# Gate and up products of a feed-forward stage, given to four PSUM banks in turn

## The chip, the cores and the metric

The kernel runs on one core of a Trainium2 chip. The metric is the time of one execution on the device in microseconds (us). Before the change three runs took 1269.52, 1270.49 and 1271.22 us, so the median is 1270.49 us. The names used for the engines are PE for TensorE (PEld for its weight loads), DVE for VectorE, ACT for ScalarE, POOL for GpSimd and SP for SyncE, which issues the weight transfers.

## The reference

The program is one inference step of a trunk of two layers, for 256 prompt tokens and 64 sample tokens (320 together) that share their weights. Each layer mixes tokens in two branches, and ends in the feed-forward part that the change is in:

```python
h = _rmsnorm(x, p['norm_ffn_pre'])
f = (jax.nn.silu(h @ p['w_ffn_gate']) * (h @ p['w_ffn_up'])) @ p['w_ffn_down']
x = x + _rmsnorm(f, p['norm_ffn_post'])
```

The model's width is 1024 and that of the feed-forward part 2816. Everything is float32.

## The kernel before

**Layout.** Features lie on the partitions and the 320 tokens on the free axis, so that a projection is a set of products of a 128x128 weight block (loaded into PE) with a 128x320 block of activations (streamed through it). The width of 1024 is 8 such blocks, k = 0 to 7, and that of 2816 is 22.

**Three products for one.** To keep float32 accuracy, a weight tile is split into a high part `w_hi`, made by ACT (line 599), and a low part `w_lo`, made by DVE (line 912), and activations likewise into `h_hi` and `h_lo`. Every block pair takes three products in the same sum: hi x hi, hi weight x lo activation, lo weight x hi activation. `parts` (line 1404) gives them in this order. A weight tile has 1024 columns, so 8 blocks and 24 products. Raw, high and low tiles lie in rings of three: SP loads a raw tile when the low part of the tile three before it has been made, and ACT makes a high part when PE has used the tile three before.

**The gate and up stage.** There are 11 quads per layer (`q` in `for q in range(FK // 2)`). A quad makes four sums of 128x320, gate, up, gate, up: group g+0, g+1, g+2, g+3. Each has a PSUM bank of its own and 24 products (8 values of k by 3). The quad consumes four weight tiles in four calls of `cycle`, each of which takes two values of k for all four sums: 24 products per cycle, 96 per quad. Within a cycle the sums are taken in the order 0, 2, 1, 3, and each gets its six products (two k, three parts) in one piece. In the first quad of a layer (`ready` is given) the order is by k first, since the activations arrive one k at a time: there each sum gets three products in one piece.

**Banks.** Seven banks go round: `wide = dense + core[1:5]`, and `bank(g)` is `wide[(g - G_GU) % 7]`. Quad 1 so has core2, core3, core4, dense0 for its sums 0 to 3, quad 2 has dense1, dense2, core1, core2. The first product into a bank waits (`open_bank`, line 1390) until the group seven before has been read out of it. For the sums 0, 1 and 2 of a quad that is a group of the quad before last; for sum 3 it is sum 0 of the quad just before.

**Reading out.** DVE multiplies each finished sum by the norm's `root` into SBUF (line 1359), in the order 0, 2, 1, 3, and counts `dense_evac_v`. The last value of k of each sum in a cycle counts `phase_done`, so a quad counts 16. `finished` (line 343) makes the reading of sums 0 and 2 wait for the 15th count of the quad, that of sums 1 and 3 for the 16th. ACT applies SiLU to the gates (line 885), and DVE multiplies by the up sum, splits the result into `f_hi` and `f_lo` (lines 1365, 939, 940), and makes low parts of four weight tiles in between. Then it waits for the next quad.

**Around it.** Behind the first quad, PE does one product with `pick` (`x_pick`), ACT makes `root` from it (lines 632, 634), and only then can DVE read out the first quad. After quad 10 the down projection uses `f_hi` and `f_lo` in 22 tiles, with all 66 products of an output group in one bank.

All matmuls are recorded at line 1388, the helper `mm`.

Of the kernel before, what the change touches and what calls it, by code (L numbers as in the profile page):

```python
# [10 lines left out]
T = TP + TS  # L11
# [11 lines left out]
T_WOA, T_WOB, T_WO, T_GU, T_DOWN, NT = 55, 59, 67, 75, 119, 141  # L23
# [123 lines left out]
def program(nc, x_t, wts, pvec, lora, shift0, fixed, rmask, trig, rconst, wkv_st, ret_d, ret_t,  # L147
# [5 lines left out]
    with ctx:  # L153
# [95 lines left out]
        def bank(g):  # L249

            if g < OPEN:
                return opened[g]
            if T_V <= g < T_GATE + 4:
                return dense[(g - T_V) % 2]
            return dense[(g - (OPEN if g < T_V else T_GATE + 4)) % 3] if g < G_GU else wide[(g - G_GU) % 7]
# [11 lines left out]
        def many(n, *names, unit=1):  # L267

            return [Signal(name, n, unit) for name in names]
# [9 lines left out]
        phase_done, = many(4 * (T_DOWN - T_GU), "phase_done")  # L279
# [53 lines left out]
        def low_ready(layer, n):  # L333

            return low_made(layer, n + 1)
# [23 lines left out]
        def evacuated_by(layer, g):  # L359

            if T_V <= g < T_GATE:
                return v_feat(layer, g - T_V + 1)
            if G_GU <= g < G_DOWN:
                g += (0, 1, -1, 0)[(g - G_GU) % 4]
            on_dve = [q < T_QK or T_GATE <= q < G_WO or G_GU <= q < G_DOWN for q in range(g + 1)]
            return dense_evac_v(layer, sum(on_dve)) if on_dve[g] else dense_evac_a(layer, sum(not v for v in on_dve) - 8 * (g >= T_GATE))
# [5 lines left out]
        def ch(t, c, lo=0, hi=T):  # L372
            return t[:, c * T + lo:c * T + hi]
# [1009 lines left out]
        def _(pe):  # L1383
            pe.wait_ge(fixed_loaded, 16)
            pe.wait_ge(pad_ready, 2)
            for layer in range(DEPTH):
                def mm(out, lhsT, rhs, start=True, stop=True):
                    return pe.matmul(out, lhsT, rhs, start=start, stop=stop)  # L1388

                def open_bank(g):  # L1390
                    if g >= G_GU + 7:
                        pe.wait_ge(*evacuated_by(layer, g - 7))
                    elif g >= G_GU:
                        pe.wait_ge(*evacuated_by(layer, G_GU - 1))
                        if g >= G_GU + 4:
                            pe.wait_ge(*ret_upd_evac(layer, 2 * HP))
                    elif g == T_GATE + 6:
                        pe.wait_ge(*seq_evac(layer, EVAC_AT["s3", SAMPLE]))
                    elif T_V + 2 <= g < T_GATE + 6:
                        pe.wait_ge(*evacuated_by(layer, g - 2))  # L1400
                    elif g >= OPEN and (V_FIRST or g not in (T_V, T_V + 1)):
                        pe.wait_ge(*evacuated_by(layer, g - (OPEN if g < OPEN + 3 else 3)))

                def parts(j, b):

                    hi, lo = w_hi[j % RING][:, b * 128:(b + 1) * 128], w_lo[j % RING][:, b * 128:(b + 1) * 128]
                    return ((hi, 0), (hi, 1), (lo, 0))
# [105 lines left out]
                def halves(out, lhsT, rhs, start=True, stop=True):  # L1513

                    mm(out[0:C], lhsT[0:C], rhs[0:C], start, stop)
                    return mm(out[C:2 * C], lhsT[C:2 * C], rhs[C:2 * C], start, stop)

                def across(out, lhsT, rhs, start=True, stop=True):

                    mm(out[C:2 * C], lhsT[0:C], rhs[0:C], start, stop)  # L1520
                    return mm(out[0:C], lhsT[C:2 * C], rhs[C:2 * C], start, stop)
# [24 lines left out]
                def product(job, m):  # L1546

                    name, lv, s = job
                    bank = round_bank(job)
                    b128 = slice((4 * s + m) * 128, (4 * s + m + 1) * 128)  # L1550
                    b64 = slice((4 * s + m) * C, (4 * s + m + 1) * C)
                    of = slice(m * C, (m + 1) * C)
                    ps, ps64 = bank[:, m * 128:(m + 1) * 128], bank[:, of]
                    turned = across if s in FLIP else halves
                    if name == "vt":
                        return across(ps64, stream(zs[:, 11 * T:15 * T], s)[:, m, :], i2)
                    if name == "mt":
                        return halves(ps, b_st[:, b64], ar[:, b128])
                    if name == "kt":
                        return across(ps, k_st[:, b64], ar[:, b128])  # L1560
                    if name == "tk":
                        return across(ps64, k_dec[:, of] if s == HP else k_st[:, b64], i2)
                    if name == "tb":
                        return halves(ps64, b_dec[:, of] if s == HP else b_st[:, b64], i2)
                    if name in ("m", "mx"):
                        return (across if name == "mx" else halves)(ps64, ar[:, b128][:, 0:C], b_st[:, b64])
                    if name == "e":
                        return turned(ps64, (p_sq[lv % 2] if lv else m_sq)[:, b64], xt[:, b64])
                    if name == "dt":
                        return turned(ps64, x_sq[:, b64], e_sq[:, b64])  # L1570
                    return halves(ps64, e_sq[:, b64], x_sq[:, b64])

                pe.wait_ge(*bonus_out(layer, HP))
                for i, slot in enumerate(ROUNDS, 1):
                    pair = [named(t) for t in slot.split()]
                    for job in pair:
                        n = JOB_AT[job] - 1
# [5 lines left out]
                    for m in range(4):  # L1583
                        for job in pair:
                            ins = product(job, m)
# [34 lines left out]
                for name, c in SEQ:  # L1620
                    w, u = (wu_s, wu_s) if c == SAMPLE else (w_st, u_st)

                    def mat(t, h, w):
                        return step_mats(t, c, w)[:, h, :]

                    def out(what, h):
                        b, o = seq_place(what, c)
                        return banks[b][:, o + h * C:o + (h + 1) * C]

                    def col(t, h):  # L1630
                        return t[:, h * C:(h + 1) * C]
# [17 lines left out]
                    if name in ("as0", "as1", "as2", "as3"):  # L1649
# [5 lines left out]
                        for s in range(NSEQ):  # L1655
# [3 lines left out]
                            ins = halves(o3[:, :, toks], col(s0_st, h * NSEQ + s), a3[:, :, toks])  # L1659
                        done(ins)  # L1660
                    elif name == "w":
# [5 lines left out]
                        for h in range(HP):  # L1667
                            beside(h)
                            if c == SAMPLE:
                                ins = halves(out("w", h), asr[:, h * 128:h * 128 + C], i2)  # L1670
                            elif c:
                                ins = halves(out("w", h), mat(ar, h, 128)[:, 0:C], col(s_st, h))
                            else:
                                ins = across(out("w'", h), mat(makt, h, C), mat(v_st, h, C))
                        done(ins)
                    elif name == "u":
                        evac("w", c)
                        for h in range(HP):
                            beside(h)
                            ins = halves(out("u", h), mat(xt, h, C), col(w, h))  # L1680
                        done(ins)
                    elif name in ("ys", "y"):
                        evac("u", c)
                        for h in range(HP):
# [4 lines left out]
                            ins = halves(out("y", h), col(u, h), mat(mrb, h, C), not state, True)  # L1689
                        if name == "ys":  # L1690
                            for h in range(HP):
                                ins = halves(out("s", h), mat(tok, h, 128)[:, C:2 * C], col(u, h))
# [72 lines left out]
                for hp in range(HP):  # L1765
                    q, k = ch(qk_rot, hp), ch(qk_rot, 4 + hp)
# [17 lines left out]
                    for u in range(2):  # L1784
                        for j in range(4):
                            of = slice((2 * j + u) * 128, (2 * j + u + 1) * 128)
                            ins = mm(core[2][32 * j:32 * j + 32, 384:512], q_exp[:, (2 * j + u) * 32:(2 * j + u + 1) * 32],
                                     old[:, of], u == 0, u == 1)
# [13 lines left out]
                    both = core[3][:, TP:TP + 2 * TS]  # L1802
# [21 lines left out]
                def cycle(n, g, k0, last, act, ready=None):  # L1824

                    pe.wait_ge(*low_ready(layer, T_GU + n))
                    both = [(one, k) for one in (0, 2, 1, 3) for k in (k0, k0 + 1)]
                    if ready:
                        both.sort(key=lambda u: u[1])
                    for one, k in both:  # L1830
                        if k == 0:
                            open_bank(g + one)
                        if ready and one == 0:
                            pe.wait_ge(*ready(layer, k))
                        for m, (w, which) in enumerate(parts(T_GU + n, 4 * (k - k0) + one)):
                            ins = mm(bank(g + one)[:, 0:T], w, ch(act[which], k), k == 0 and m == 0, k == last and m == 2)
                        if k == k0 + 1:
                            ins.then_inc(phase_done.sem, 1)

                for q in range(FK // 2):  # L1840
                    for i in range(4):
                        cycle(4 * q + i, G_GU + 4 * q, 2 * i, KT - 1, (h_hi, h_lo),
                              (lambda layer, k: h_ready(layer, KT + k + 1)) if q == 0 else None)
                        if q == 0 and i in (1, 2):
                            x_sum(2, i - 1)
                        if q == 0 and i == 3:
                            x_pick(2)
# [149 lines left out]
```

## Time and profile before

| what | us |
|---|---|
| median of three runs | 1270.49 |
| span of the profiled execution | 1270.8 |
| PE busy | 1221.7 (96% of the span) |
| PE weight loads busy | 1157.7 (91%) |
| DVE busy | 855.3 (67%) |
| ACT busy | 558.2 (44%) |
| PE busy from 416 to 558 us (quads 1 to 10 of the first layer) | 141.58 of 142.00 |

For the profiled execution the page gives the span only; it lies 0.3 us above the median and inside the three runs. Busy means that an instruction is in the engine, and products overlap each other in PE: a 128x320 product is recorded as 0.31 us long, while the next starts about 0.147 us after it. What a product costs is therefore the distance between two starts. Where PE waits, the row of the product carries the idle time and the engine that ended it in square brackets.

### The profile page before, as it was taken

To read this page: it belongs to the slowest core of one execution; us is meant where nothing else is said; L and a number is where in the kernel's file an instruction comes from. 1 tells how busy PE (TensorE), PEld (TensorE's weight loads), DVE (VectorE), ACT (ScalarE), POOL (GpSimd) and SP (SyncE) were. 2 spreads that over 40 slices of the span, in tenths; PEclk is the share of its full clock that TensorE was granted. 3 is DMA by queue.
4 is the path that set the end of the run, shared out by engine and by line. 5 is a ranking of instruction groups with operands and counts; after the bars stand their busy time and mean duration, and the time that the engine had idled before them with its cause. 6 is when DMAs were issued, how large, how long until landed. Compare 5 with 4: busy or idle time off the path is not lost.

```text
span 1270.8 us, 27906 instructions
## 1 busy us (share of the span) xinstructions
PE 1221.7 (96%) x12056; PEld 1157.7 (91%) x12056; DVE 855.3 (67%) x1468; ACT 558.2 (44%) x849; POOL 152.7 (12%) x168
## 2 busy tenths in 40 slices
PE   6999899999999999999989998999999999999996
PEld 5999788998998999999978987889999989999996
DVE  4887558878776666663378864687878576666433
ACT  4553345455536333343355544444563453333432
POOL 0004456100000000000000062840100000000000
PEclk9999899999999999999999999999999999999999
DMA  6433144644453644444424432364444535444441
GB/s 215 143 116 122 40 118 146 250 127 144 123 166 102 221 150 150 150 149 150 150 91 126 134 100 74 103 212 172 148 159 135 163 107 166 152 143 154 153 149 67
DMA packets 51466, 179.13 MB, mean 141 GB/s; under 512 B 6288, under 2 KB 7568, under 8 KB 50064
## 3 DMA queue, kind: packets, MB, share of 16 engines
q1 hardware_dynamic: 42576, 153.77, 38.5%
q10 hardware_dynamic: 8768, 23.58, 5.2%
q8 instruction: 95, 1.56, 0.5%
q14 instruction: 27, 0.22, 0.1%
HBM read 166.18 MB, written 8.53 MB: 137 GB/s over the span
## 4 chain that ended last, share of the span: by engine, by line
PE 83%; DVE 9%; ACT 4%; issue 2%; DMA 1%; ACTq 0%; SPq 0%; DVEq 0%
PE dense L1388 52%; PE core L1388 31%; DVE w_lo L912 2%; ACT w_hi L599 1%; DVE x L962 1%; DVE y_out L960 1%; DMA ret_s<-ret_t 1%; DMA x<-x_t 0%; ACT L587 0%; DVE ret_t L1257 0%; DVE bonus L1031 0%; DVE tmp L1017 0%; ACT sq_pair L822 0%; ACT h_hi L605 0%; DVE bonus L1027 0%
## 5 line engine op out<-in xcount | busy, mean ns | idle before, releaser
L912 DVE TENSOR_TENSOR w_lo<-w_raw,w_hi 128x1024 fp32r<-128x1024 f32 x282 | 352.7, 1253 | 220.1 <-ACT w_hi L599 219.5
L599 ACT ACTIVATE w_hi<-w_raw 128x1024 fp32r<-128x1024 f32 x282 | 297.6, 1057 | 415.5 <-PE dense L1388 273.3
L1388 PE MATMUL dense<-h_hi,w_hi 128*128 128x320 f32 x1296 | 415.3, 320 | 20.1 <-DVE w_lo L912 11.3
L1388 PE MATMUL dense<-h_lo,w_hi 128*128 128x320 f32 x1296 | 403.0, 311 | 0.0
L1388 PE MATMUL dense<-h_hi,w_lo 128*128 128x320 f32 x1296 | 402.8, 311 | 0.0
L1388 PEld LDWEIGHTS dense<-h_hi,w_hi 128*128 128x128 f32 x1296 | 245.5, 189 | 40.2 <-issue 30.8
L1388 PEld LDWEIGHTS dense<-h_lo,w_hi 128*128 128x128 f32 x1296 | 245.9, 190 | 1.3 <-issue 0.2
L1388 PEld LDWEIGHTS dense<-h_hi,w_lo 128*128 128x128 f32 x1296 | 245.7, 190 | 0.0
L1388 PE MATMUL core<-h_hi,w_hi 128*128 128x320 f32 x416 | 129.3, 311 | 0.4 <-DVE w_lo L912 0.4
L1388 PE MATMUL core<-h_hi,w_lo 128*128 128x320 f32 x416 | 128.7, 309 | 0.0
L1388 PE MATMUL core<-h_lo,w_hi 128*128 128x320 f32 x416 | 128.7, 309 | 0.0
L1388 PEld LDWEIGHTS core<-h_hi,w_hi 128*128 128x128 f32 x416 | 78.2, 188 | 0.8 <-DVE w_lo L912 0.7
L1388 PEld LDWEIGHTS core<-h_lo,w_hi 128*128 128x128 f32 x416 | 78.2, 188 | 0.2
L1388 PEld LDWEIGHTS core<-h_hi,w_lo 128*128 128x128 f32 x416 | 78.2, 188 | 0.0
L491 POOL TENSOR_TENSOR xt<-xt,fx 128x256 f32<-128x256 f32 x10 | 7.4, 736 | 558.0 <-DVE xt L1085 558.0
L587 ACT ACT_TABLE_LOAD x31 | 39.8, 1283 | 34.7 <-DMA ret_s<-ret_t 16.2
L1388 PE MATMUL dense<-f_hi,w_hi 128*128 128x320 f32 x176 | 54.2, 308 | 0.0
L1388 PE MATMUL core<-f_lo,w_hi 128*128 128x320 f32 x176 | 54.2, 308 | 0.0
L1388 PE MATMUL core<-f_hi,w_lo 128*128 128x320 f32 x176 | 54.2, 308 | 0.0
L1388 PE MATMUL core<-f_hi,w_hi 128*128 128x320 f32 x176 | 54.2, 308 | 0.0
L1388 PE MATMUL dense<-f_lo,w_hi 128*128 128x320 f32 x176 | 54.2, 308 | 0.0
L1388 PE MATMUL dense<-f_hi,w_lo 128*128 128x320 f32 x176 | 54.2, 308 | 0.0
(306 smaller groups left out, 1994.1 us busy)
## 6 DMA issues: line engine op xcount, KB each, us to landing
w_raw<-wts SPq DMA_DIRECT2D x282, 512.0 KB, 3.5
ret_t<-ret_t ACTq DMA_DIRECT2D x16, 256.0 KB, 3.4
ret_s<-ret_t ACTq DMA_DIRECT2D x16, 256.0 KB, 2.4
ret_rest<-ret_d ACTq DMA_DIRECT2D x2, 1536.0 KB, 8.2
qk_rot<-qk_raw SPq DMA_DIRECT2D x8, 320.0 KB, 6.4
dmask<-rconst ACTq DMA_DIRECT2D x2, 1152.0 KB, 5.4
s_st<-wkv_st ACTq DMA_DIRECT2D x2, 1024.0 KB, 4.9
wkv_s<-s_st ACTq DMA_DIRECT2D x2, 1024.0 KB, 4.3
```

Of the source, the lines that this page charges most:

```text
L491: return pool.tensor_tensor(pairs(t, s, C), pairs(t, s, C), bc(i2, 1, 4), ALU.add)
L587: act.preload_act_table_set(name)
L599: act.activation(w_hi[n % RING][:, :], w_raw[n % RING][:, :], ACT.Copy).then_inc(hi_ready.sem, 1)
L912: dve.tensor_tensor(w_lo[r][:, :], w_raw[r][:, :], w_hi[r][:, :].bitcast(F32), ALU.subtract).then_inc(low_made.sem, 1)
L960: link(dve.tensor_tensor(y.rearrange("p (c t) -> p c t", t=T), y.rearrange("p (c t) -> p c t", t=T), bc(root[:, :], 1, hi - lo), ALU.mult))
L962: dve.tensor_tensor(xs, xs, y, ALU.add).then_inc(added.sem, 1)
L1388: return pe.matmul(out, lhsT, rhs, start=start, stop=stop)
```

## The change

In `cycle` the loops change places. For each of the two values of k, and for each of the three parts, the four sums get one product each, in the order 0, 2, 1, 3. The number of products, their operands and the order within one sum stay; so do the wait for the weight tile at the head of a cycle and the wait for the activations at the head of each k. The wait that opens a bank stands as before in front of the first product into it, and the `phase_done` counts stand behind the last product of each sum in a cycle.

```diff
-                    both = [(one, k) for one in (0, 2, 1, 3) for k in (k0, k0 + 1)]
-                    if ready:
-                        both.sort(key=lambda u: u[1])
-                    for one, k in both:
-                        if k == 0:
-                            open_bank(g + one)
-                        if ready and one == 0:
+                    for k in (k0, k0 + 1):
+                        if ready:
                             pe.wait_ge(*ready(layer, k))
-                        for m, (w, which) in enumerate(parts(T_GU + n, 4 * (k - k0) + one)):
-                            ins = mm(bank(g + one)[:, 0:T], w, ch(act[which], k), k == 0 and m == 0, k == last and m == 2)
-                        if k == k0 + 1:
-                            ins.then_inc(phase_done.sem, 1)
+                        for m in range(3):
+                            for one in (0, 2, 1, 3):
+                                if k == 0 and m == 0:
+                                    open_bank(g + one)
+                                w, which = parts(T_GU + n, 4 * (k - k0) + one)[m]
+                                ins = mm(bank(g + one)[:, 0:T], w, ch(act[which], k), k == 0 and m == 0, k == last and m == 2)
+                                if k == k0 + 1 and m == 2:
+                                    ins.then_inc(phase_done.sem, 1)
```

The instruction lists of DVE, ACT and SP stay as they are. On PE, here is the place where quad 1 of the first layer ends and quad 2 begins, in the kernel before. Quad 1 ends with six products into dense0 (its sum 3), and the last into core3 (its sum 1) is the row ahead of them; quad 2 comes to core2, which holds sum 0 of quad 1, with its 19th product.

```order
L1388 MATMUL core3<-h_hi,w_lo1 128x320
L1388 MATMUL dense0<-h_hi,w_hi1 128x320
L1388 MATMUL dense0<-h_lo,w_hi1 128x320
...
L1388 MATMUL dense0<-h_hi,w_lo1 128x320
L1388 MATMUL dense1<-h_hi,w_hi2 128x320 [waits dense_evac_v,low_made]
L1388 MATMUL dense1<-h_lo,w_hi2 128x320
...
L1388 MATMUL dense2<-h_hi,w_lo2 128x320
L1388 MATMUL core2<-h_hi,w_hi2 128x320 [waits dense_evac_v]
```

The same place after the change, with no row left out:

```order
L1388 MATMUL core2<-h_hi,w_lo1 128x320
L1388 MATMUL core4<-h_hi,w_lo1 128x320
L1388 MATMUL core3<-h_hi,w_lo1 128x320
L1388 MATMUL dense0<-h_hi,w_lo1 128x320
L1388 MATMUL dense1<-h_hi,w_hi2 128x320 [waits dense_evac_v,low_made]
L1388 MATMUL core1<-h_hi,w_hi2 128x320 [waits dense_evac_v]
L1388 MATMUL dense2<-h_hi,w_hi2 128x320 [waits dense_evac_v]
L1388 MATMUL core2<-h_hi,w_hi2 128x320 [waits dense_evac_v]
```

The last product into core3, with the 15th count, has moved from the seventh place before the end of the quad to the second, and the first product into core2, with the wait for its being read, from the 19th place of the next quad to the fourth.

At the end of quad 0 the kernel before goes on, behind `pick`, with six products into core2, six into core4 and six into core3, and then comes to dense0, which holds sum 0 of quad 0. After the change it reads:

```order
L1388 MATMUL core1<-h_hi,w_lo0 128x320
L1388 MATMUL core0<-acc_141,fx 128x320 [waits x_parted]
L1388 MATMUL core2<-h_hi,w_hi1 128x320 [waits ret_upd_evac,dense_evac_a,low_made]
L1388 MATMUL core4<-h_hi,w_hi1 128x320 [waits ret_upd_evac,dense_evac_a]
L1388 MATMUL core3<-h_hi,w_hi1 128x320 [waits ret_upd_evac,dense_evac_a]
L1388 MATMUL dense0<-h_hi,w_hi1 128x320 [waits dense_evac_v]
L1388 MATMUL core2<-h_lo,w_hi1 128x320
```

Here too the product that waits for DVE's reading of dense0 has moved from the 19th place to the fourth.

## Rows read from the trace of the kernel before

**Rows 1.** The page, parts 1 and 4: busy times, and shares of the chain.

```profile
PE 1221.7 (96%) x12056; PEld 1157.7 (91%) x12056; DVE 855.3 (67%) x1468; ACT 558.2 (44%) x849; POOL 152.7 (12%) x168
...
PE dense L1388 52%; PE core L1388 31%; DVE w_lo L912 2%; ACT w_hi L599 1%; DVE x L962 1%; DVE y_out L960 1%; DMA ret_s<-ret_t 1%; DMA x<-x_t 0%; ACT L587 0%; DVE ret_t L1257 0%; DVE bonus L1031 0%; DVE tmp L1017 0%; ACT sq_pair L822 0%; ACT h_hi L605 0%; DVE bonus L1027 0%
```

**Rows 2.** Stretches, gate and up: length, busy PE, PEld, DVE, ACT, POOL, clock, DMA.

```profile
416.00:558.00 142.00, 141.58 (x964) 141.16 (x963) 90.64 (x142) 52.54 (x64) 0.00 (x0) 1.00 0.52 162
1040.00:1181.00 141.00, 141.00 (x962) 140.84 (x961) 90.20 (x141) 52.29 (x63) 0.00 (x0) 1.00 0.48 154
```

**Rows 3.** PE timeline, first products of quads 2 and 3: start, duration, instruction.

```profile
431.10 0.31 PE L1388 MATMUL dense<-h_hi,w_hi 128*128 128x320 f32 x1
...
445.18 0.31 PE L1388 MATMUL core<-h_hi,w_hi 128*128 128x320 f32 x1
```

**Rows 4.** PE timeline in the down projection, two products 96 apart.

```profile
1195.88 0.31 PE L1388 MATMUL core<-f_hi,w_hi 128*128 128x320 f32 x1
...
1209.96 0.31 PE L1388 MATMUL core<-f_hi,w_hi 128*128 128x320 f32 x1
```

**Rows 5.** PE timeline in quad 0, where a bank ends and another begins.

```profile
400.53 0.31 PE L1388 MATMUL dense<-h_lo,w_hi 128*128 128x320 f32 x1
400.68 0.31 PE L1388 MATMUL dense<-h_hi,w_lo 128*128 128x320 f32 x1
400.82 0.31 PE L1388 MATMUL core<-h_hi,w_hi 128*128 128x320 f32 x1
```

**Rows 6.** PE timeline at the end of quad 2 and the head of quad 3.

```profile
444.16 0.31 PE L1388 MATMUL dense<-h_hi,w_lo 128*128 128x320 f32 x1
...
444.89 0.31 PE L1388 MATMUL core<-h_lo,w_hi 128*128 128x320 f32 x1
...
445.62 0.31 PE L1388 MATMUL core<-h_hi,w_hi 128*128 128x320 f32 x1
```

**Rows 7.** DVE timeline around the same place and on through quad 3.

```profile
443.02 1.23 DVE L912 TENSOR_TENSOR w_lo<-w_raw,w_hi 128x1024 fp32r<-128x1024 f32 x1 [2.29 <-ACT w_hi L599]
444.57 0.49 DVE L1359 TENSOR_TENSOR silu_g<-dense,root 128x320 f32<-128x320 f32 x1 [0.33 <-PE dense L1388]
...
453.58 1.23 DVE L912 TENSOR_TENSOR w_lo<-w_raw,w_hi 128x1024 fp32r<-128x1024 f32 x1 [2.29 <-ACT w_hi L599]
```

**Rows 8.** DVE's waits over the whole span: us in total, times, longest.

```profile
DVE silu_g L1359 <- ACT root L634: 5.0, 2, 3.0
DVE silu_g L1359 <- PE core L1388: 4.0, 12, 0.3
DVE silu_g L1359 <- PE dense L1388: 2.6, 8, 0.3
```

**Rows 9.** Timeline of DVE, PE and PEld where PE waits for `w_lo` in quad 1.

```profile
422.68 1.23 DVE L912 TENSOR_TENSOR w_lo<-w_raw,w_hi 128x1024 fp32r<-128x1024 f32 x1 [1.85 <-ACT w_hi L599]
...
423.23 0.31 PE L1388 MATMUL dense<-h_hi,w_lo 128*128 128x320 f32 x1
...
423.96 0.19 PEld L1388 LDWEIGHTS core<-h_hi,w_hi 128*128 128x128 f32 x1 [0.69 <-DVE w_lo L912]
...
424.21 0.31 PE L1388 MATMUL core<-h_lo,w_hi 128*128 128x320 f32 x1
```

**Rows 10.** Timeline of PE, ACT and DVE at the head of quad 1, first layer.

```profile
416.78 0.31 PE L1388 MATMUL core<-h_hi,w_hi 128*128 128x320 f32 x1
...
417.10 0.47 ACT L634 ACTIVATE root<-root 128x320 f32<-128x320 f32 x1
...
417.60 0.89 DVE L1359 TENSOR_TENSOR silu_g<-dense,root 128x320 f32<-128x320 f32 x2 [1.96 <-ACT root L634]
```

**Rows 11.** Timeline of PE and DVE at the same place of the second layer.

```profile
1041.00 0.31 PE L1388 MATMUL core<-h_hi,w_hi 128*128 128x320 f32 x1
...
1041.82 0.89 DVE L1359 TENSOR_TENSOR silu_g<-dense,root 128x320 f32<-128x320 f32 x2 [3.03 <-ACT root L634]
```

**Rows 12.** Stretches with and without a lowered clock, columns as in rows 2.

```profile
146.00:150.00 4.00, 1.68 (x67) 1.38 (x66) 1.06 (x3) 1.16 (x4) 0.00 (x0) 0.88 0.03 8
150.00:154.00 4.00, 4.00 (x69) 3.67 (x72) 0.66 (x3) 0.00 (x0) 0.00 (x0) 0.50 0.02 4
154.00:158.00 4.00, 4.00 (x125) 3.74 (x119) 2.93 (x6) 1.32 (x4) 0.00 (x0) 0.77 0.15 12
396.00:412.00 16.00, 14.00 (x102) 11.52 (x98) 13.67 (x21) 10.87 (x22) 0.00 (x0) 1.00 0.16 54
```

## The prediction

> **What bounds the kernel now.** I read the page first. PE is busy for 1221.7 of 1270.8 us, and 83% of the chain that ended last are its products [rows 1]. The table by stretches then says what holds in the stage that changes: from quad 1 on PE is busy for 141.58 of 142.00 us in the first layer and for all of 141.00 in the second, at a granted clock of 1.00, and DVE for 90 to 91 [rows 2]. The stage is a row of products with nothing between them, so its time is their number times their distance, plus what PE waits. The PE timeline gives the distance: quad 2 starts at 431.10 and quad 3 at 445.18, so 96 products take 14.08 us, or 0.1467 us each [rows 3]. Two things can change it: another distance, or new waits. For the waits I read the timelines of PE and DVE around the end of a quad, where DVE has to read a bank that PE wants again.
>
> **The distance of two products: nothing.** The change adds no product and no weight load. It changes the bank with each product, 96 times a quad, where it was 16 times (every sixth). Whether a change of bank costs or saves can be read from stages that change it at other rates. In the down projection 66 products in a row go to one bank, and 96 of them take 1209.96 - 1195.88 = 14.08 us [rows 4], the same as with 16 changes. Inside quad 0, which changes every third product, the step across a change (400.68 to 400.82) is 0.14 us and that inside a bank (400.53 to 400.68) 0.15 us [rows 5], equal within the 0.01 us of the rows. So 16 changes against one or two make less than 0.01 us, or under 0.001 us per change. The change adds 80 in each of 20 quads and 64 in each of the two first (which go from 32 to 96), 1728 in all: at 0.001 us that is 1.7 us to either side, and I take 0. No row has a change at every product, so this is an extrapolation, and its failure is a rival.
>
> **The wait at the fourth product of a quad: +0.32 us, 18 times.** Two things move toward each other. DVE reads sum 0 when the 15th count of the quad has come. That count is now on the last product of sum 1, the 18th of 24 in the last cycle; it starts at 444.16 [rows 6], and DVE, which has been idle for 0.33 us, starts to read at 444.57 [rows 7], 0.41 us later. After the change the 15th count is on the 23rd product, five places later, which starts at 444.89 [rows 6]. DVE will then start at 444.89 + 0.41 = 445.30 and, with a reading of 0.49 us [rows 7], end at 445.79. The bank of sum 0 is needed by sum 3 of the next quad. Now that is its 19th product, 15 places or 2.2 us after the fourth, and never late; after the change it is the fourth, due at 445.62 [rows 6]. So it is late, and I need what a wait costs beyond the moment of release. PE's wait for `w_lo` shows it: DVE ends at 422.68 + 1.23 = 423.91, the weight load starts at 423.96, and the product after the released one starts at 424.21, so the released one holds the place of 424.21 - 0.15 = 424.06 [rows 9]: 0.15 us behind DVE's end, since the weight load is held up too. The fourth product is worth 445.79 + 0.15 = 445.94 instead of 445.62, a loss of 0.32 us. The bounds: if DVE starts earlier by 0.07 (it wakes sooner behind a stream of counts) and the weight load is not held up (0.05 in place of 0.15), the loss is 0.15; if DVE needs 0.1 more, it is 0.42.
>
> How often: DVE waits for PE ahead of this reading 12 + 8 = 20 times, never by less than the rest, 6.6 us in all or 0.33 each [rows 8]. These are quads 1 to 10 of both layers; DVE is thus on time at every one. Quad 10 is followed by the down projection, which comes to that bank much later; quads 1 to 9 pay: 18 x 0.32 = 5.8 us (2.7 to 7.6).
>
> Behind DVE's reading wait SiLU on ACT and the split of `f` and the next low parts on DVE, all some 0.73 us later than now (five products). It is hidden: later in the quad DVE idles for 2.29 us ahead of a `w_lo`, for a high part that ACT can make only when PE has used a tile [rows 7]. And the last `f` blocks are wanted by the down projection 60 and more products (8.8 us) after the quad's end.
>
> **The first quad: +1.46 us in the second layer, +0.78 in the first.** Here the reading waits not for PE but for `root`, which ACT makes from the product behind quad 0. DVE reads sum 0 from 417.60 on, for 0.49 us, until 418.09 [rows 7, 10]. Neither moves. PE's fourth product of quad 1 stands at 416.78 [rows 10] and now goes into a bank that is free; after the change it wants the bank of sum 0 and gets it at 418.09 + 0.15 = 418.24. The loss is 1.46 us. In the second layer: 1041.82 + 0.49 + 0.15 - 1041.00 = 1.46 us [rows 11]. In the first layer PE loses time in this quad already: after 423.23 the next product is due at 423.38 and holds the place of 424.06 because `w_lo` is late, 0.68 us [rows 9]. That low part waits for ACT, behind SiLU and transfers which all hang on the same reading of quad 0 and don't move; PE, 1.46 us later, finds it ready. So the first layer pays 1.46 - 0.68 = 0.78 us.
>
> **Sum.** 5.8 + 1.46 + 0.78 = 8.0 us. PE is the end of the chain behind the stage too (down projection, next layer), so nothing takes it back. The profiled span of 1270.8 lies 0.3 above the median of 1270.49; on the median that gives 1278.5 us. The likeliest case's own range, from the bounds of the steady wait and of the first quads (0.1 each way), is 1275 to 1280.5 us.
>
> **Rivals.**
> *The products come closer together.* If giving each product another bank than its neighbour lets it start earlier, all 2112 products gain. 320 columns at 2.4 GHz, the level of a granted clock of 1.00 [rows 2], are 133.3 ns, against a distance of 146.7: up to 13.3 x 2112 = 28 us less. With the waits that is 1270.5 + 8 - 28 = 1250 us; a third of it is enough for "faster". Against it: steps across a bank's change are no shorter than others [rows 5], nor are they in the down stage longer [rows 4]. Chance 6%. The Trainium skill ("TensorE: Matmul & The Clock Gate", Back-to-back issue gap) gives N / 2.4 + 2.5 ns for isolated products, 136 ns here; by it alone, with the distance falling to that, the gain would be an estimated 23 us, but no run here shows that distance.
>
> *The steady wait does not bind*, because the count wakes DVE sooner or the load is taken ahead. Then only the first quads pay: 1270.5 + 2.2 = 1272.7 us. It needs 0.32 us less on a chain that the rows give in four steps of 0.41, 0.49, 0.05 and 0.10. Chance 8%.
>
> *PE's clock falls.* If a stop at each of 20 heads of quads let the granted clock fall to 0.50 for a while, each would cost some 3 us: around 150 us it stands at 0.50 and 0.77 for 8 us, that is 2.0 + 0.9 = 2.9 us lost [rows 12]. That gives 1270.5 + 8 + 20 x 2.9 = 1337 us. It would take idle stretches like those from 146 to 150, where PE is busy for 1.68 of 4.00 us; from 396 to 412 PE stands idle for 2 us of 16 and the clock stays at 1.00 [rows 12]. Chance 2%. The Trainium skill (the same page, "A second HAM failure mode: psum-queue depth-cycling") speaks directly against this change: cycling through banks with small idle times between groups made the clock go up and down in one kernel. Quad 0, with a change at every third product and waits between them, keeps its clock in this trace, so I give the rule little.
>
> **Chances and range.** The forecast has 80%, shorter distance 6%, no steady wait 8%, clock 2%, and 4% is for larger waits than I bound (1281 to 1285 us). A difference of 0.2%, 2.5 us, is what a measurement can tell from no change. The forecast, the clock and the larger waits are slower by more; of the case at 1272.7 some falls within it. Slower 0.88, same 0.06, faster 0.06. The range 1272.5 to 1281.5 us takes in the case without a steady wait and leaves out both outer rivals.
>
> **What would show it.** In the changed kernel's profile the fourth product of quads 2 to 10 should carry a wait of about 0.2 us on DVE's line 1359, some 0.32 us more between quad starts (14.40 for 14.08), and the fourth of quad 1 one of about 1.4 us. DVE's reading of sum 0 should start 0.41 us after the start of the last-but-one product of a quad. The distance of two products inside a quad should stay at 0.147 us, the clock at 1.00, and the 0.68 us lost to `w_lo` in the first layer should be gone. A distance under 0.145 us, or no wait on line 1359 in the steady quads, would make the prediction wrong.

## The result, and the profile after

The changed kernel's median is 1279.55 us (1276.81 to 1282.53, four runs), that of the kernel before, measured beside it, 1270.01 us (1268.01 to 1271.22). The ratio is 1.0079, with a 95% interval of 1.0058 to 1.0100, so 10.0 us slower (7.4 to 12.8). Forecast were 8.0 us and 1278.5 us. The ratio is an estimate from all the runs and not the quotient of the two medians, which lie 9.5 us apart; in the experiments below the two also differ, by up to 1.4 us, and it is the ratio with its interval that counts.

The profiled execution spans 1276.2 us, only 5.4 us more than that of before. Where the time went is therefore read from the gate and up stage itself. DVE's readings of sum 0 mark the quads. Here they are at the heads of the two stages and at the end of quads 2 and 3 (columns: start, duration, instruction, idle time before it and who ended it):

```profile
414.83 0.89 DVE L1359 TENSOR_TENSOR silu_g<-dense,root 128x320 f32<-128x320 f32 x2 [1.96 <-ACT root L634]
...
429.24 0.89 DVE L1359 TENSOR_TENSOR silu_g<-core,root 128x320 f32<-128x320 f32 x2 [1.06 <-PE core L1388]
...
443.64 0.49 DVE L1359 TENSOR_TENSOR silu_g<-dense,root 128x320 f32<-128x320 f32 x1 [1.06 <-PE dense L1388]
...
458.05 0.49 DVE L1359 TENSOR_TENSOR silu_g<-core,root 128x320 f32<-128x320 f32 x1 [1.06 <-PE core L1388]
...
1042.77 0.89 DVE L1359 TENSOR_TENSOR silu_g<-dense,root 128x320 f32<-128x320 f32 x2 [2.97 <-ACT root L634]
...
1057.18 0.89 DVE L1359 TENSOR_TENSOR silu_g<-core,root 128x320 f32<-128x320 f32 x2 [1.06 <-PE core L1388]
```

From 443.64 to 458.05 it is 14.41 us, where [rows 3] have 14.08. DVE's idle time ahead of a reading was 0.33 us [rows 7] and is 1.06 us: 0.73 us more, the five products by which the 15th count has moved. The timeline of PE, PEld and DVE at the end of quad 2 shows where the 0.33 us are lost; it answers to [rows 6, 7]:

```profile
443.23 0.31 PE L1388 MATMUL dense<-h_hi,w_lo 128*128 128x320 f32 x1
...
443.37 0.31 PE L1388 MATMUL core<-h_hi,w_lo 128*128 128x320 f32 x1
...
443.52 0.31 PE L1388 MATMUL core<-h_hi,w_hi 128*128 128x320 f32 x1
...
443.64 0.49 DVE L1359 TENSOR_TENSOR silu_g<-dense,root 128x320 f32<-128x320 f32 x1 [1.06 <-PE dense L1388]
443.67 0.31 PE L1388 MATMUL dense<-h_hi,w_hi 128*128 128x320 f32 x1
...
443.81 0.31 PE L1388 MATMUL core<-h_hi,w_hi 128*128 128x320 f32 x1
...
444.19 0.19 PEld L1388 LDWEIGHTS dense<-h_hi,w_hi 128*128 128x128 f32 x1 [0.33 <-DVE silu_g L1359]
444.19 0.41 PE L1388 MATMUL dense<-h_hi,w_hi 128*128 128x320 f32 x1
...
444.44 0.30 PE L1388 MATMUL core<-h_lo,w_hi 128*128 128x320 f32 x1
```

The last-but-one product of the quad starts at 443.23. DVE starts to read 0.41 us later and ends at 444.13. The quad's fourth product was due at 443.96; its weight load starts at 444.19, and its successor at 444.44, so the fourth product holds the place of 444.29: 0.33 us late. The wait stands in the row of the weight load, not in that of the product, whose record starts 0.07 us after its predecessor's ends (443.81 + 0.31) and carries no wait.

All of it in one table of waits (us in total, times, longest): first for the product rows, then for the weight loads.

```profile
PE dense L1388 <- DVE silu_g L1359: 2.4, 2, 1.2
```

```profile
PEld dense L1388 <- DVE silu_g L1359: 5.6, 10, 1.5
...
PEld core L1388 <- DVE silu_g L1359: 3.3, 10, 0.3
```

Twenty weight loads wait for line 1359, none did before: 18 of 0.33 us and two, at the heads of the quads 1, of 1.5 us. Only these two show in the product rows too, with 1.2 us each.

**The sum, from reading to reading.** Besides the readings at 417.60 and 1041.82 in [rows 10, 11] and those above, it needs the second and the last of each layer before, and the last of each layer after:

```profile
430.49 0.89 DVE L1359 TENSOR_TENSOR silu_g<-core,root 128x320 f32<-128x320 f32 x2 [0.33 <-PE core L1388]
...
557.21 0.49 DVE L1359 TENSOR_TENSOR silu_g<-core,root 128x320 f32<-128x320 f32 x1 [0.33 <-PE core L1388]
...
1054.03 0.89 DVE L1359 TENSOR_TENSOR silu_g<-core,root 128x320 f32<-128x320 f32 x2 [0.33 <-PE core L1388]
...
1180.75 0.49 DVE L1359 TENSOR_TENSOR silu_g<-core,root 128x320 f32<-128x320 f32 x1 [0.33 <-PE core L1388]
```

```profile
558.94 0.49 DVE L1359 TENSOR_TENSOR silu_g<-core,root 128x320 f32<-128x320 f32 x1 [1.06 <-PE core L1388]
...
1186.91 0.49 DVE L1359 TENSOR_TENSOR silu_g<-core,root 128x320 f32<-128x320 f32 x1 [1.06 <-PE core L1388]
```

Over the ten steps of a layer the readings of sum 0 span 139.61 and 138.93 us before, 144.11 and 144.14 us after. Of each difference 0.73 us is only the later reading in the last quad. That leaves 3.77 and 4.48 us, 8.25 us together. By steps: the nine steady ones take 14.41 for 14.08 us (18 x 0.33 = 6.0 us), the first ones 14.41 for 12.89 and 14.41 for 12.21, which without the 0.73 is 0.79 and 1.47 us.

**Why the profiled spans differ by 5.4 only.** The first reading of the stage falls at 414.83, 2.77 us earlier than the 417.60 of [rows 10], though no instruction ahead of it has changed. In the profile of before the clock fell twice ahead of the stage, around 150 and around 300 us. The rows of stretches around 150 us (length, busy time of PE, PEld, DVE, ACT, POOL, granted clock, DMA) show the first fall by its absence; this is the profile after, the kernel before is in [rows 12]:

```profile
146.00:150.00 4.00, 2.51 (x119) 2.12 (x111) 1.18 (x3) 1.71 (x6) 0.00 (x0) 1.00 0.13 52
150.00:154.00 4.00, 4.00 (x169) 3.63 (x167) 2.29 (x7) 0.89 (x3) 0.00 (x0) 1.00 0.01 4
154.00:158.00 4.00, 3.86 (x155) 3.53 (x158) 1.85 (x4) 1.83 (x7) 0.00 (x0) 1.00 0.40 135
```

The second is in these rows, before and then after:

```profile
296.00:300.00 4.00, 2.65 (x33) 1.83 (x33) 3.79 (x9) 1.10 (x2) 0.00 (x0) 0.90 0.62 194
300.00:304.00 4.00, 4.00 (x17) 3.21 (x16) 3.69 (x11) 1.16 (x2) 0.00 (x0) 0.67 0.84 277
```

```profile
296.00:300.00 4.00, 3.78 (x39) 2.84 (x40) 3.83 (x9) 0.47 (x1) 0.00 (x0) 1.00 0.50 173
300.00:304.00 4.00, 4.00 (x29) 4.00 (x29) 3.58 (x11) 2.16 (x3) 0.00 (x0) 1.00 0.95 337
```

Reckoned like the 2.9 us of the first (0.50 and 0.77 for 8 us), the second fall comes to 0.4 + 1.3 = 1.7 us. The lead of 2.77 us is not simply their sum: followed along the same instructions, the execution after is 0.8 us behind at 135 us, then ahead by about 3.1 at 190, 1.1 at 280 and 2.8 from 318 on. Both falls add to it; what takes back some 2 us in between stays open. For the spans only the lead itself matters, since it arose before the stage: 8.25 - 2.77 = 5.5 us, against 5.4 between the spans.

### The profile page after: what moved, and what is told of

It reads as the page before. It is cut to its first block, busy times and chain, and to the rows that moved or that the text cites. A ratio compares the mean times of both kernels' runs of the same rounds, so it can differ in the third digit from the quotient of the medians.

```text
span 1276.2 us, 27906 instructions
## 1 busy us (share of the span) xinstructions
PE 1224.3 (96%) x12056; PEld 1155.1 (91%) x12056; DVE 854.3 (67%) x1468; ACT 558.4 (44%) x849; POOL 152.5 (12%) x168
## 4 chain that ended last, share of the span: by engine, by line
PE 83%; DVE 10%; ACT 4%; issue 2%; DMA 1%; ACTq 0%; SPq 0%; DVEq 0%
PE dense L1388 51%; PE core L1388 31%; DVE w_lo L912 2%; ACT w_hi L599 1%; DVE x L962 1%; DVE silu_g L1359 1%; DVE y_out L960 1%; DMA ret_s<-ret_t 1%; DMA x<-x_t 0%; ACT L587 0%; DVE ret_t L1257 0%; DVE bonus L1031 0%; DVE tmp L1017 0%; ACT sq_pair L822 0%; ACT h_hi L605 0%
## 5 line engine op out<-in xcount | busy, mean ns | idle before, releaser
L1388 PE MATMUL dense<-h_hi,w_hi 128*128 128x320 f32 x1296 | 399.5, 321 | 22.9 <-DVE w_lo L912 11.3
L1388 PE MATMUL dense<-h_hi,w_lo 128*128 128x320 f32 x1296 | 385.8, 311 | 0.0
L1388 PE MATMUL dense<-h_lo,w_hi 128*128 128x320 f32 x1296 | 385.8, 311 | 0.0
L1388 PEld LDWEIGHTS dense<-h_hi,w_hi 128*128 128x128 f32 x1296 | 241.1, 189 | 44.7 <-issue 29.5
L1388 PE MATMUL core<-h_hi,w_hi 128*128 128x320 f32 x416 | 106.6, 313 | 0.7
L1388 PE MATMUL core<-h_hi,w_lo 128*128 128x320 f32 x416 | 104.3, 309 | 0.0
L1388 PE MATMUL core<-h_lo,w_hi 128*128 128x320 f32 x416 | 104.3, 309 | 0.0
L1388 PEld LDWEIGHTS core<-h_hi,w_hi 128*128 128x128 f32 x416 | 72.5, 188 | 3.6 <-DVE silu_g L1359 3.3
L1388 PEld LDWEIGHTS core<-h_lo,w_hi 128*128 128x128 f32 x416 | 72.4, 188 | 0.0
L1388 PEld LDWEIGHTS core<-h_hi,w_lo 128*128 128x128 f32 x416 | 72.3, 188 | 0.0
```

## The experiments

Three theories went into them, and the kernels take the 24 products of a cycle from two lists: `turn` has them in the order of the changed kernel, `pieces` in that of the kernel before. The diffs are shortened. The theory: a bank is wanted again before it has been read out. Rival A: the turns themselves make products dearer. Rival B: DVE's work behind the readings comes late, and PE pays for that somewhere. "Reading to reading" is the distance of DVE's readings of sum 0, in a steady quad; "extra in the first step" is its length over that of before (12.89 and 12.21 us), with the shift of the reading (0.73 us, or 0.88 with the 16th count) taken off where there is one. Ratios are to the kernel before, run beside.

| kernel | ratio (95% interval) | reading to reading | extra in the first step, layers 1 and 2 |
|---|---|---|---|
| before | 1 | 14.08 | 0, 0 |
| changed, again | 1.0061 (1.0038 to 1.0083) | 14.41 | 0.79, 1.47 |
| pieces in the last cycle | 1.0013 (0.9996 to 1.0031) | 14.08 | 0.78, 1.46 |
| pieces in the first cycle | 0.9999 (0.9982 to 1.0015) | 14.08 | -0.11, 0.01 |
| changed, reads at the 16th count | 1.0082 (1.0056 to 1.0108) | 14.56 | 0.79, 1.47 |
| before, reads at the 16th count | 1.0001 (0.9987 to 1.0015) | 14.08 | -0.13, 0.00 |
| sum 3 opens at the tenth product | 1.0016 (1.0004 to 1.0029) | 14.08 | -0.10, 0.59 |
| turns with an eighth bank | 1.0003 (0.9992 to 1.0013) | 14.08 | 0.27, 0.94 |

### The changed kernel again

> The changed kernel, run again beside the others of this group. Theory (a late bank): each of quads 1 to 9 of both layers loses 0.32 us at its successor's fourth product, which waits until DVE has read sum 0, and the first quads lose 1.46 and 0.78 us: 8.0 us over the kernel before, 14.40 us from quad to quad. Rival A (the turns themselves): the products lie further apart by 8.0 us / 1728 added changes of bank = 4.6 ns each, so the distance is 0.151 us and there is no stop at the fourth product.

Measured: 1277.10 us against 1269.39, ratio 1.0061 or 7.7 us. The second profile has the same steps as the first:

```profile
447.12 0.49 DVE L1359 TENSOR_TENSOR silu_g<-dense,root 128x320 f32<-128x320 f32 x1 [1.06 <-PE dense L1388]
...
461.54 0.49 DVE L1359 TENSOR_TENSOR silu_g<-core,root 128x320 f32<-128x320 f32 x1 [1.06 <-PE core L1388]
```

The distance of two products can be taken from the first profile of the changed kernel: from the fifth product of quad 3, at 444.44, to the first of quad 4, 92 products on, all with a bank other than their neighbour's.

```profile
457.93 0.31 PE L1388 MATMUL dense<-h_hi,w_hi 128*128 128x320 f32 x1
```

13.49 / 92 = 0.1466 us, as before. Rival A wants 0.151. It falls here already.

### Pieces in the last cycle: the count goes back, the early opening stays

```diff
-                    for k in (k0, k0 + 1): ...   # turns in every cycle
+                    for one, k, m in pieces if k0 == 6 else turn:
```

> The last cycle of each quad is put back in pieces of six products per sum, the other three stay in turns. The 15th count is on the 18th product again, but the bank of sum 0 is still wanted at the fourth product of the next quad. Theory: DVE reads sum 0 from 0.61 us before the quad's end to 0.12 us before it, 0.56 us before the fourth product: no wait in the steady quads (14.08 us each); only the first quads lose 1.46 + 0.78 us, since their reading waits for root: +2.2 us over the kernel before. Rival A (the turns themselves): three quarters of the changes of bank stay, so about three quarters of the loss, +6 us. Rival B (what DVE does behind the readings comes late): gone too, as in the theory, but without the 2.2 us.

Measured: 1271.07 us against 1269.39, +1.7 us (-0.5 to +3.9). The timed ratio separates this from the changed kernel's 7.7 us, but hardly from nothing; the profile has the 2.2 us. Readings of the quads 0 and 1 of the second layer, then of quads 2 and 3 of the first:

```profile
1038.32 0.89 DVE L1359 TENSOR_TENSOR silu_g<-dense,root 128x320 f32<-128x320 f32 x2 [1.96 <-ACT root L634]
...
1051.99 0.89 DVE L1359 TENSOR_TENSOR silu_g<-core,root 128x320 f32<-128x320 f32 x2 [0.33 <-PE core L1388]
...
441.48 0.49 DVE L1359 TENSOR_TENSOR silu_g<-dense,root 128x320 f32<-128x320 f32 x1 [0.33 <-PE dense L1388]
...
455.56 0.49 DVE L1359 TENSOR_TENSOR silu_g<-core,root 128x320 f32<-128x320 f32 x1 [0.33 <-PE core L1388]
```

The steady quads are at 14.08, with DVE idle 0.33 us as before; the first step is 13.67 against 12.21 us, 1.46 more. The steady loss needs the late count; the first quads' loss doesn't, as it should be where the reading waits for `root`. Rival A's +6 us lies outside the interval.

### Pieces in the first cycle: the opening goes back, the late count stays

```diff
-                    for k in (k0, k0 + 1): ...
+                    for one, k, m in pieces if k0 == 0 else turn:
```

> The first cycle of each quad is put back in pieces, the other three stay in turns. The bank of sum 0 is wanted at the 19th product of the next quad again, the 15th count stays on the 23rd of the cycle, so DVE reads and does all its later work of a quad 0.73 us late. Theory: the reading ends 0.61 us after the quad's end, the bank is wanted 2.6 us after it: no wait anywhere, 14.08 us from quad to quad, the first quads lose nothing: 0 us against the kernel before (within 1 us). Rival A (the turns themselves): +6 us. Rival B (DVE's work comes late): that is unchanged, so the whole loss stays, +8 us.

Measured: 1270.65 us against 1269.39, ratio 0.9999, between 2.3 us faster and 1.9 slower.

```profile
444.83 0.49 DVE L1359 TENSOR_TENSOR silu_g<-dense,root 128x320 f32<-128x320 f32 x1 [1.07 <-PE dense L1388]
...
458.91 0.49 DVE L1359 TENSOR_TENSOR silu_g<-core,root 128x320 f32<-128x320 f32 x1 [1.06 <-PE core L1388]
```

DVE idles 1.06 us and reads as late as in the changed kernel, and three cycles of four take turns; the quad takes 14.08 us. That is against both rivals at once. The -0.11 us of the first layer in the table, like the -0.13 with the 16th count below, lies in the wait for `w_lo`: its weight load waits 0.56 us in both, where [rows 9] have 0.69. Why that wait is shorter was not tried.

### The reading at the 16th count

```diff
-                return phase_done(layer, end - 1 if (g - G_GU) % 2 == 0 else end)
+                return phase_done(layer, end)
```

In the changed kernel:

> The changed kernel, with the reading of sums 0 and 2 waiting for the 16th count in place of the 15th, which comes one product (0.147 us) later. Theory: every steady quad loses 0.147 us more: 14.55 us from quad to quad, 18 x 0.147 = 2.6 us over the changed kernel and 10.7 us over the kernel before; the first quads don't move, their reading waits for root. Rival A (the turns themselves): no change against the changed kernel. Rival B: the delay of DVE's work grows from 0.73 to 0.88 us, a fifth, so 1.6 us.

Measured: 1280.75 us against 1269.39, ratio 1.0082 or 10.4 us (7.1 to 13.7), where 10.7 was forecast. Against the changed kernel's 7.7 us of the same group the timed intervals overlap; the profile is sharp:

```profile
444.16 0.49 DVE L1359 TENSOR_TENSOR silu_g<-dense,root 128x320 f32<-128x320 f32 x1 [1.21 <-PE core L1388]
...
458.73 0.49 DVE L1359 TENSOR_TENSOR silu_g<-core,root 128x320 f32<-128x320 f32 x1 [1.21 <-PE dense L1388]
```

14.57 us here (14.56 in the mean of the steps) for 14.41: one product's distance of delay in the count is one product's distance in every quad. In the kernel before the same edit is six products of delay:

> The kernel before (products in pieces), with the reading of sums 0 and 2 waiting for the 16th count in place of the 15th: six products, 0.88 us, later. Theory: the reading then ends 0.76 us after the quad's end, the bank is wanted at the 19th product, 2.64 us after it: no wait, 0 us (within 1 us), though DVE's later work is all 0.88 us late. Rival B (DVE's work comes late): at least the 8 us of the changed kernel, whose delay is 0.73 us.

Measured: 1269.88 us against 1269.82, ratio 1.0001 (1.9 us to either side at most).

```profile
441.51 0.49 DVE L1359 TENSOR_TENSOR silu_g<-dense,root 128x320 f32<-128x320 f32 x1 [1.21 <-PE core L1388]
...
455.59 0.49 DVE L1359 TENSOR_TENSOR silu_g<-core,root 128x320 f32<-128x320 f32 x1 [1.21 <-PE dense L1388]
```

The idle time of DVE is the same 1.21 us, and the quad takes 14.08 us. DVE's later work as such, 0.88 us late, costs nothing. Rival B is out.

### Sum 3 opens at the tenth product

Against the changed kernel:

```diff
+                    late = sorted(turn[0:12], key=lambda u: u[0] == 3) + turn[12:]
-                    for k in (k0, k0 + 1): ...
+                    for one, k, m in late if k0 == 0 else turn:
```

> The changed kernel, with one thing moved: at the head of each quad, for the first value of k, the three products of sum 3 come behind the nine of the sums 0, 2 and 1, which take turns. The bank of sum 0 is wanted at the tenth product in place of the fourth, 0.88 us later; everything else is as in the changed kernel. Theory: the steady quads have 0.88 us more room against a loss of 0.32: no wait, 14.08 us each. The first quads lose 1.46 - 0.88 = 0.58 us: in the second layer in full, in the first it takes the place of as much of the 0.68 us that PE loses there to w_lo: +0.6 us over the kernel before. Rival A (the turns themselves): nearly all 8 us stay. Rival B (DVE's work comes late): all 8 us stay.

Measured: 1271.71 us against 1269.82, ratio 1.0016 or 2.0 us (0.5 to 3.7), where 0.6 was forecast. The changed kernel's loss is outside the interval, 0.6 at its lower end. By the profile it is -0.10 + 0.59 = 0.5 us; what the timed median has beyond that is not explained by any step of this stage. Readings of quads 0 and 1 of the second layer, and of quads 2 and 3 of the first:

```profile
1038.35 0.89 DVE L1359 TENSOR_TENSOR silu_g<-dense,root 128x320 f32<-128x320 f32 x2 [2.79 <-ACT root L634]
...
1051.88 0.89 DVE L1359 TENSOR_TENSOR silu_g<-core,root 128x320 f32<-128x320 f32 x2 [1.06 <-PE core L1388]
...
441.23 0.49 DVE L1359 TENSOR_TENSOR silu_g<-dense,root 128x320 f32<-128x320 f32 x1 [1.06 <-PE dense L1388]
...
455.31 0.49 DVE L1359 TENSOR_TENSOR silu_g<-core,root 128x320 f32<-128x320 f32 x1 [1.06 <-PE core L1388]
```

Six products of room take off 0.88 us of the 1.47 us of the first quad (13.53 - 12.21 - 0.73 = 0.59), and all of the 0.33 us of the others. In the first layer the wait of 0.59 us stands in place of the 0.69 us for `w_lo`, hence the -0.10.

### Full turns with an eighth bank

```diff
-        wide = dense + core[1:5]
+        wide = dense + core[1:5] + core[0:1]
-            return ... wide[(g - G_GU) % 7]
+            return ... wide[(g - G_GU) % 8]
-                    if g >= G_GU + 7:
-                        pe.wait_ge(*evacuated_by(layer, g - 7))
+                    if g >= G_GU + 8:
+                        pe.wait_ge(*evacuated_by(layer, g - 8))
+                    elif g == G_GU + 7:
+                        pe.wait_ge(*x_rooted(layer, 2))
```

> The changed kernel with full turns and an eighth bank in the round: core0, which holds the product behind quad 0 until ACT has made root from it, is sum 3 of quad 1 and then goes round with the others. A bank is then wanted by the quad after next, for sum 3 too. The order of the products is that of the changed kernel. Theory (a late bank): no wait in the steady quads, 14.08 us each, though the bank changes with every product; in quad 1 the fourth product waits for root instead of for DVE's reading behind it: root ends at 417.10 + 0.47 = 417.57, 0.15 us later is 417.72, against 416.78: 0.94 us in the second layer, and 0.94 - 0.68 = 0.26 us in the first: +1.2 us over the kernel before. Rival A (the turns themselves): all 8 us stay, since the turns are unchanged. Rival B (DVE's work comes late, by 0.73 us, as in the changed kernel): all 8 us stay.

Measured: 1270.53 us against 1269.29, ratio 1.0003, +0.4 us (-1.0 to +1.7), where 1.2 was forecast. By the profile it is 0.27 + 0.94 = 1.2 us. The interval holds both this and zero; the changed kernel's loss is far outside it. The wait of the weight load at the head of quad 1, second layer, is on `root` now, and the steady quads are free:

```profile
1044.58 0.19 PEld L1388 LDWEIGHTS core<-h_hi,w_hi 128*128 128x128 f32 x1 [0.94 <-ACT root L634]
```

```profile
444.39 0.89 DVE L1359 TENSOR_TENSOR silu_g<-dense,root 128x320 f32<-128x320 f32 x2 [1.06 <-PE dense L1388]
...
458.46 0.89 DVE L1359 TENSOR_TENSOR silu_g<-core,root 128x320 f32<-128x320 f32 x2 [1.06 <-PE core L1388]
```

This kernel issues the same products in the same order as the changed one, with a bank changed at every product, and has 14.08 us per quad. In the steady quads the turns as such cost nothing and bring nothing. No version measured is faster than the kernel before.

## Why the prediction was right

**The distance of two products: 0.** Right. It had been carried over from stages that change the bank after 3, 6 and 66 products; at every product it is 0.1466 us. The bound of 1.7 us was not needed.

**The wait at the fourth product: 0.32 us, 18 times.** Measured 0.33, 18 times, 6.0 us for 5.8. Each step of it can be found again: count to reading 0.41 us, reading 0.49, DVE's end to weight load 0.06, and the place of the product 0.10 behind the start of its load. The two experiments that undo one movement each show that it takes both, and the 16th count that the loss grows by what the count is late. In one detail I was wrong: I had expected a wait of about 0.2 us in the product's row, and one of 1.4 in quad 1. The steady one is in the weight load's row alone, as 0.33; that of quad 1 is 1.5 us there and 1.2 in the product's row.

**The first quads: 1.46 and 0.78 us.** Measured 1.47 and 0.79. That the first layer takes back 0.68 us is seen in the kernels of the table too: the steps of the two layers are 12.89 and 12.21 us before, but 14.41 and 14.41 in the changed kernel, and 13.67 and 13.67 with pieces in the last cycle. PE's wait for `w_lo` there is hidden behind the new one: between 412 and 432 us the weight loads of the changed kernel wait for line 1359 and for nothing else.

**What was costed at nothing.** DVE's work behind the readings comes 0.73 us late, and 0.88 with the 16th count in the kernel before, and nobody waits for it. The down projection starts without a wait: the step sum of 8.25 us, less the 2.77 us by which the two executions differ ahead of the stage, is the difference of the spans to 0.1 us.

**The rivals.** Products closer together, and no steady wait: both excluded by the rows. (The prediction's remark that a third of the 28 us would be enough for "faster" was wrong by its own numbers: 9.3 us against 8 of waits leave 1.3, less than the 2.5 that a measurement can tell.) The clock's fall: from quad 1 on it was granted at 1.00 throughout, with a stop of 0.33 us every 14.4 us. Here are the stretches of the two layers in the changed kernel, columns as in [rows 2]:

```profile
416.00:558.00 142.00, 141.40 (x950) 139.04 (x949) 88.23 (x138) 50.09 (x61) 0.00 (x0) 1.00 0.49 158
...
1040.00:1186.00 146.00, 144.20 (x965) 141.40 (x964) 89.49 (x140) 52.40 (x63) 0.00 (x0) 1.00 0.46 149
```

The case of the Trainium skill ("TensorE: Matmul & The Clock Gate", A second HAM failure mode: psum-queue depth-cycling) is thus not this one, though the kernel cycles through its banks and stops between quads. One reason for the low chance did not hold, however. The prediction says that quad 0 keeps its clock, and looked at the first layer only. At the same place of the second layer, in the same trace of the kernel before, the clock fell (first the row of the first layer, then two of the second):

```profile
396.00:400.00 4.00, 2.20 (x18) 1.25 (x15) 3.05 (x6) 3.54 (x7) 0.00 (x0) 1.00 0.20 82
...
1020.00:1024.00 4.00, 2.20 (x11) 1.74 (x9) 3.87 (x8) 2.72 (x5) 0.00 (x0) 0.86 0.02 6
1024.00:1028.00 4.00, 4.00 (x22) 4.00 (x21) 3.54 (x7) 1.73 (x4) 0.00 (x0) 0.72 0.00 0
```

It falls there after the change too (0.98 and 0.60), so the difference of the two kernels has nothing of it. That this rival deserved its low chance is shown by the quads 1 to 10, not by quad 0.

The first of the two long rows also shows how little the busy share tells: PE is busy for 141.40 us of it, against 141.58 before, with 1.5% fewer records of products (950 for 964), and by the steps each quad takes 2.3% longer. PEld, 139.04 for 141.16, shows the stops.

The timed difference of 10.0 us (7.4 to 12.8), and 7.7 (4.8 to 10.5) in the second group, hold the forecast 8.0 and the profile's 8.25.

## What to carry to other kernels

Issuing sums in turns makes them all finish at the end and all begin at the start: it shortens, from both sides, the way from the product whose count lets DVE read a bank to that bank's next first product, here from 25 products to five. Five are 0.73 us, and the start of the reading, the reading and the restart need 0.41 + 0.49 + 0.16 = 1.06. Count, for the bank that comes round soonest, the products from the count that releases its reader to its next opening, and hold against that the reader's start, its duration and the restart of the stalled product. If it is short, another bank in the round or a later opening of that one sum gives the time back, as shown here; where the products already follow each other at one distance whatever the bank, turns have nothing to bring.

## What the runs showed of the hardware

A change of bank with every 128x320 product, against one in 66, moves the distance of two products by less than 0.001 us (0.1466 us at 92 products with turns, 14.08 / 96 without). With the eighth bank, where nothing waits, 96 products in turns take the same 14.08 us.

DVE starts its reading 0.41 to 0.42 us after the start of the product with the count, in all 20 readings of the kernel before and wherever the rows of the changed one show that product by itself.

The granted clock in an unchanged stretch differs from one execution to the next: around 150 us it fell to 0.50 in the profiled execution of before and not in that of the changed kernel. Ahead of the fall PE was busy for 1.68 of 4 us, in the execution without it for 2.51 of 4. Why PE had less to do there was not tried. PE's busy time in one such stretch doesn't tell by itself whether the clock will fall: around the start of quad 0, in the trace of before, it was busy for 2.20 of 4 us in both layers (from 396 and from 1020 us on), and the clock fell only in the second.

Executions with a lower mean clock tend to be the longer ones. Of the 17 timed executions of the kernel before that ran beside the eighth bank, the three at 0.990 took 1271.9 to 1272.9 us, the two at 0.995 took 1267.5 and 1268.5. In another group of 23 the same tendency is weak, so the clock is one part of the spread and how large a part is open.
